# Seventeen of thirty modulation units summed by VectorE straight from the weight ring

## The chip, the cores and the metric

The kernel runs on one core of a Trainium2 chip. The metric is the time of one execution on the device in microseconds (us). Engines are named as in the profile: PE is TensorE, DVE is VectorE, ACT is ScalarE, POOL is GpSimd, SP is SyncE, which issues most of the loads. PEld is PE's loading of weights.

## The reference

All numbers are f32, x has 256 tokens of 1024 channels. Two layers are followed by one block of another kind. Each takes its shifts, scales and gates from one conditioning vector c:

```python
for layer in range(2):
    mod = silu(c) @ w_ada[layer] + b_ada[layer]          # (1024,) @ (1024, 6144)
    sh1, sc1, g1, sh2, sc2, g2 = split(mod, 6)
    h = rms_norm(x, norm1_g) * (1 + sc1) + sh1
    # layer 0: dilated attention (8 heads) beside a gated unit (gMLP); layer 1: a convolution
    # (31 taps) beside stick-breaking attention (8 heads)
    x = x + g1 * (mix(h) @ w_out)
    h = rms_norm(x, norm2_g) * (1 + sc2) + sh2
    x = x + g2 * hierarchical_moe(h)                     # 16 experts of 3 x 2 MB, 2 per token
x = rms_norm(x, final_norm_g)
shift, scl, gate = split(silu(c_2) @ w_c_2 + b_c_2, 3)   # (1024,) @ (1024, 3072)
h = rms_norm(x, g_pre) * (1 + scl) + shift
proj = h @ w_in                                          # (1024, 8192)
# a recurrence and a neighbourhood attention of 16 heads, merged; then
x = rms_norm(x + gate * (merged @ w_o), g_final)
```

## The kernel before

**The ring.** Every large weight is cut into units of 2 MB: 1024 rows by 512 columns, or one of the three matrices of an expert. `stream()` lists all 162 units in the order of loading. SP loads them into a ring of six slots; unit n goes into slot n mod 6, and its load waits until unit n-6 has been read, which PE told with the semaphore `unit_done`. A dense unit is read by `by_channel` (L456) or `by_token` (L469).

**The modulation units.** The three products of a vector with a matrix are 30 such units, ada0 to ada29: ada0 to 11 are layer 0, 12 to 23 layer 1, 24 to 29 the last block. For each, `ada_main` (L492) runs eight matmuls of the conditioning vector, repeated 32 times, against the eight row blocks of the unit, four beside each other in the array; the profile counts an f32 matmul as two instructions, so a unit is x16. ACT copies the bank to SBUF (`ada_part_copy`, L1173). `ada_columns` (L505) then sums over the partitions and turns 512 sums into four columns, by four matmuls of one column each (x8), and DVE adds the bias (`ada_cols`, L1539, `mod<-bank,cv`), which counts `ada_ready` up. PE, ACT and DVE each run their own instructions in the order in which the code stands; a wait holds all that stands behind it.

**Where they stand.** ada0 to 3 come first. ada4 and ada5 are run between the projections ev0, ev1 and ev2 of layer 0. ada6 to 16 are run inside the loop over the eight dilated heads, one in each head and a second in the last ones (from `TWO_A`). Per head PE computes scores (L596, L597), DVE the maximum (L1542 on the bank), ACT the exponential (L1202), DVE sum and division, PE turns the result (L629), ACT copies it (L1231), PE multiplies with the values (L643, L644), ACT evicts the output (L1238). Two banks of scores are in turn, so the scores of head h+2 wait for the output of head h, and ACT runs the exponential of head h+1 before the copy of head h. ada17 to 22 stand in the routing of layer 0 (two behind the projection evo1, four in `experts`), ada23 in layer 1 behind the projection od4, ada24 to 29 in the routing of layer 1.

**Routing and experts.** `routed_norm` and `experts` turn x, compute the logits (L672, L679) and rank the tokens (L691 to L695). Then eight pairs of experts run, each with 192 matmul instructions of 32 columns (L751); they gather tokens (L723) and scatter results (L772).

**POOL** writes a few vectors to DRAM and reads them back in another layout: `broadcast_gate(n)` for the gate of the mixing part, and `affine_by_row(layer)` for scale and shift of the second norm (L2481 and L2484), which `tile_out` (L1125) waits for. The convolution of layer 1 is 31 taps on DVE (L1539, 128x256).

## Time and profile before

| | us |
|---|---|
| median of three runs | 1268.32 |
| lowest, highest | 1265.24, 1273.74 |
| the profiled execution | 1266.25 |
| its span, first to last instruction | 1264.5 |
| PE busy | 1198.5 |
| PE busy with L492 / with L505 | 64.3 / 30.8 |
| DVE busy | 361.2 |
| DMA read | 350.8 MB |

The page cuts the span into 40 slices of 31.6 us. Layer 0 up to its experts takes slices 0 to 6, its experts 7 to 14, the mixing part of layer 1 slices 15 to 18, its experts 20 to 26, the last block the rest.

### The profile page before, as it was taken

The numbers are of one execution on the slowest core, as the hardware profiler recorded it, in microseconds if no ns is written. First come the engines' busy times: TensorE is split into PE (matmuls) and PEld (weight loads), VectorE is DVE, ScalarE is ACT, GpSimd is POOL, SyncE is SP. The second block draws the span as 40 slices with busy tenths as digits, with TensorE's granted clock in tenths as the row PEclk, the third lists the DMA queues.
The fourth block names the chain that finished last, engine by engine and source line by source line (L and its number), as shares of the span: only waits on it lengthen the run. The fifth ranks groups of instructions, "written<-read, shape, count | busy, mean of one in ns | idle before, by whom it ended". The sixth has DMA issues, their size and how long they took to land.

```text
span 1264.5 us, 17438 instructions
## 1 busy us (share of the span) xinstructions
PE 1198.5 (95%) x7154; PEld 702.5 (56%) x7155; DVE 361.2 (29%) x1017; ACT 295.0 (23%) x626; POOL 83.8 (7%) x141
## 2 busy tenths in 40 slices
PE   4799999999999999999889999999999999999997
PEld 1566644544444448764433444445878778767773
DVE  0202414322212123952521121114211344342212
ACT  2112433111000021063400000103002545542101
POOL 2000011000000001500000000000000313200000
PEclk8799999899999999999989999999999999999999
DMA  9997999999999999831889999999834433424000
GB/s 336 313 387 243 308 280 385 382 425 428 430 429 428 429 397 208 247 133 67 360 355 404 404 422 429 427 429 388 204 133 146 152 97 130 150 80 145 17 1 33
DMA packets 90371, 352.77 MB, mean 279 GB/s; under 512 B 5284, under 2 KB 7500, under 8 KB 78028
## 3 DMA queue, kind: packets, MB, share of 16 engines
q1 hardware_dynamic: 83160, 340.68, 71.6%
q0 software_dynamic: 5488, 8.12, 3.1%
q10 hardware_dynamic: 1668, 3.21, 0.7%
q8 instruction: 38, 0.62, 0.2%
q14 instruction: 17, 0.14, 0.0%
HBM read 350.84 MB, written 1.15 MB: 278 GB/s over the span
## 4 chain that ended last, share of the span: by engine, by line
PE 80%; DMA 13%; DVE 2%; ACT 2%; issue 2%; SPq 1%; ACTq 0%; DVEq 0%
PE bank L456 28%; PE bank L751 20%; PE bank L469 12%; DMA ring<-in_moe_w_up 10%; PE bank L723 3%; PE bank L492 3%; PE bank L772 3%; DMA ring<-in_ev_w_in 2%; PE bank L505 2%; PE bank L1016 1%; SPq L368 1%; PE bank L603 1%; PE bank L640 1%; PE bank L643 1%; PE bank L629 1%
## 5 line engine op out<-in xcount | busy, mean ns | idle before, releaser
L456 PE MATMUL bank<-arena,ring 128*128 128x256 f32 x1600 | 356.0, 384 | 6.1 <-DVE arena L1539 2.8
L751 PE MATMUL bank<-ring,arena 128*32 128x512 f32 x3072 | 339.5, 600 | 12.1 <-issue 7.1
L456 PEld LDWEIGHTS bank<-arena,ring 128*128 128x128 f32 x1600 | 305.7, 192 | 54.6 <-issue 7.1
L751 PEld LDWEIGHTS bank<-ring,arena 128*32 128x32 f32 x3072 | 102.0, 111 | 237.0 <-issue 234.3
L469 PE MATMUL bank<-ring,arena 128*128 128x512 f32 x352 | 153.7, 594 | 2.3 <-DVE arena L2378 1.5
L469 PEld LDWEIGHTS bank<-ring,arena 128*128 128x128 f32 x352 | 66.2, 190 | 83.0 <-issue 79.6
L492 PE MATMUL bank<-ring,c_rep 128*32 128x512 f32 x480 | 64.3, 667 | 11.8 <-DMA ring<-in_w_ada 10.1
L2003 DVE TENSOR_TENSOR arena<-arena,bank 128x512 f32<-128x512 f32 x16 | 11.0, 688 | 203.8 <-PE bank L751 203.8
L723 PEld LDWEIGHTS bank<-arena 128*128 128x128 f32 x512 | 60.3, 197 | 13.6 <-issue 13.3
L723 PE MATMUL bank<-arena 128*128 128x128 f32 x512 | 63.4, 284 | 1.6 <-DVE arena L1971 1.5
L1283 ACT ACTIVATE arena<-bank 128x512 f32<-128x512 f32 x16 | 9.6, 597 | 216.8 <-PE bank L751 216.8
L1179 ACT ACTIVATE arena<-bank 128x512 f32<-128x512 f32 x41 | 23.6, 593 | 150.8 <-PE bank L456 121.9
L1539 DVE SCALAR_TENSOR_TENSOR arena<-arena,cv 128x256 f32<-128x256 f32 x144 | 58.3, 476 | 0.3
L772 PE MATMUL bank<-arena 128*128 128x512 f32 x128 | 57.7, 594 | 0.0
L1275 ACT ACTIVATE arena<-bank,mod,gs 128x128 f32<-128x128 f32 x64 | 24.1, 456 | 124.9 <-PE bank L723 124.9
L1542 DVE CUSTOM_DVE_ANT_1 arena<-bank,arena 128x256 f32<-128x256 f32 x32 | 12.3, 423 | 137.4 <-PE bank L604 137.4
L1107 ACT ACTIVATE arena<-x 128x512 f32<-128x512 f32 x20 | 12.5, 626 | 116.0 <-DVE x L1728 99.5
L492 PEld LDWEIGHTS bank<-ring,c_rep 128*32 128x32 f32 x480 | 14.6, 117 | 42.7 <-issue 31.9
L1989 DVE TENSOR_SCALAR arena<-bank,gs,mod 128x128 f32<-128x128 f32 x64 | 21.9, 404 | 50.3 <-PE bank L723 50.3
L772 PEld LDWEIGHTS bank<-arena 128*128 128x128 f32 x128 | 23.2, 191 | 23.0 <-issue 23.0
L1238 ACT COPY arena<-bank 64x256 f32<-64x256 f32 x32 | 11.7, 366 | 99.5 <-PE bank L641 92.2
L1539 DVE SCALAR_TENSOR_TENSOR mod<-bank,cv 128x4 f32<-128x4 f32 (+1 forms) x22 | 3.5, 161 | 101.0 <-PE bank L505 98.8
(300 smaller groups left out, 926.5 us busy)
## 6 DMA issues: line engine op xcount, KB each, us to landing
ring<-in_moe_w_gate SPq DMA_DIRECT2D x32, 2048.0 KB, 14.0
ring<-in_moe_w_up SPq DMA_DIRECT2D x32, 2048.0 KB, 16.7
ring<-in_moe_w_down SPq DMA_DIRECT2D x32, 2048.0 KB, 13.8
ring<-in_w_ada SPq DMA_DIRECT2D x24, 2048.0 KB, 14.1
ring<-in_w_in SPq DMA_DIRECT2D x16, 2048.0 KB, 8.9
ring<-in_w_c SPq DMA_DIRECT2D x6, 2048.0 KB, 9.2
ring<-in_ev_w_in SPq DMA_DIRECT2D x5, 2048.0 KB, 20.2
ring<-in_od_w_in SPq DMA_DIRECT2D x5, 2048.0 KB, 19.6
```

The lines of the kernel that those rows point to most:

```text
L368: eng.dma_start(stage[r % P:r % P + n, r // P, :], src).then_inc(sem(f"{which}_loaded"), 16)
L456: mm = pe.matmul(ps[k0][:, t * S:(t + 1) * S], w[:, k, c:c + P], rhs[:, k, :], start=(k == 0), stop=(k == KT - 1))
L469: mm = pe.matmul(ps[k0][:, :], lhs[:, k, b * P:(b + 1) * P], w[:, k, :], start=(i == 0), stop=(i == KT - 1))
L492: mm = pe.matmul(bank[32 * g:32 * g + 32, :], c_rep[:, n // (2 * ADA_SEG), 4 * r + g, :], w[:, 4 * r + g, :], start=(r == 0), stop=(r == 1 ...
L505: mm = pe.matmul(cols[:, c:c + 1], part[:, c * P:(c + 1) * P], ones[:, 0:1], start=True, stop=True)
L723: mm = pe.matmul(ps[6 + b][:, (k % 4) * P:(k % 4 + 1) * P], xn[:, t, k * P:(k + 1) * P], pick[:, t, :], start=(t == 0), stop=(t == TT - 1))
L751: mm = pe.matmul(bank[col:col + CHUNK, :], lhs[:, k, col:col + CHUNK], ring[:, s0 + e, cut], start=start, stop=stop, tile_position=(0, col))
L772: mm = pe.matmul(ps[2 * t + half][:, :], g_cur[:, t * P:(t + 1) * P], y_pair[:, half * 512:(half + 1) * 512], start=False, stop=True, skip ...
L1179: act.activation(dst, v, func, scale=scale).then_inc(free, 1)
L1275: ins = act.activation(x_cur[:, k, :], ps[6][:, k * P:(k + 1) * P], ACT.Identity, bias=mod[:, sh + k:sh + k + 1], scale=gs[:, 2 * layer + ...
L1539: return dve.scalar_tensor_tensor(out_, in0, scalar, in1, op0, op1)
L1989: ins = dve.tensor_scalar(x_cur[:, k, :], ps[7][:, (k - 4) * P:(k - 3) * P], gs[:, 2 * layer + 1, 0, k:k + 1], mod[:, sh + k:sh + k + 1], ...
```

## The change

Seventeen units (4 to 11, 17 to 23, 28 and 29) are no longer read by PE. DVE reads them in the ring: `modulate` multiplies each of the eight row blocks with its value of the conditioning vector and adds up, eight dependent instructions of 128x512. PE is left with the sum over the partitions, now from DVE's result (`summed_columns`, several units in a row), and DVE adds the bias for several units at once (`summed_cols`). The slot of such a unit is free when DVE has summed it (`read_wait`). The other thirteen units stay with PE: 0 to 3, five in the routing of layer 0 (12 to 16, six before), four in that of layer 1 (24 to 27, six before). The order of loading changes with them: before the experts of layer 0 stand 24 units where there were 30.

```diff
-    u += [("ev", 0), ("ada", 4), ("ev", 1), ("ada", 5), ("ev", 2)]
-    u += [("ev", 4), ("ada", 6), ("ev", 3), ("ada", 7)]
-    u += [("ada", n) for n in range(8, 17)]
+    u += [("ev", 0), ("ada", 4), ("ev", 1), ("ada", 5), ("ada", 6), ("ev", 2), ("ada", 7)]
+    u += [("ev", 4), ("ada", 8), ("ev", 3), ("ada", 9), ("ada", 10), ("ada", 11)]
     u += [("evo", 0), ("evo", 1)]
-    u += [("ada", n) for n in range(17, 23)]
+    u += [("ada", n) for n in range(12, 17)]
     u += [("moe", 0)] * (6 * PAIRS)
-    u += [("od", i) for i in range(5)]
-    u += [("ada", 23), ("odo", 0), ("odo", 1)]
-    u += [("ada", n) for n in range(24, 30)]
+    u += [("od", 0)] + [("ada", n) for n in range(17, 21)]
+    u += [("od", i) for i in range(1, 5)]
+    u += [("ada", n) for n in range(21, 24)]
+    u += [("odo", 0), ("odo", 1)]
+    u += [("ada", n) for n in range(24, 28)]
     u += [("moe", 1)] * (6 * PAIRS)
-    u += [("in", n) for n in (0, 1, 4, 6, 8, 2, 3, 10, 11, 12, 13, 5, 7, 9, 14, 15)]
+    u += [("in", 0), ("in", 1), ("ada", 28), ("ada", 29)]
+    u += [("in", n) for n in (4, 6, 8, 2, 3, 10, 11, 12, 13, 5, 7, 9, 14, 15)]
+SUMMED = tuple(range(4, 12)) + tuple(range(17, 24)) + (28, 29)
-        ROUTE_UNITS = ((17, 6), (24, 6))
+        ROUTE_UNITS = ((12, 5), (24, 4))
-        ROUTE_SOON = 3
+        ROUTE_SOON = (4, 3)
...
+            def summed_columns(lo, hi, base=None):
+                base = lo if base is None else base
+                if lo == base:
+                    pe.wait_ge(sem("ada_ready"), lo)
+                for n in range(lo, hi):
+                    pe.wait_ge(sem("modulation_summed"), summed_at(unit_of[f"ada{n}"]))
+                    part = sum_of(n)
+                    for c in range(4):
+                        o = 4 * (n - base) + c
+                        mm = pe.matmul(ps[4][:, o:o + 1], part[:, c * P:(c + 1) * P], ones[:, 0:1],
+                                       start=True, stop=True)
+                    mm.then_inc(sem("ada_cols_full"), 1)
+                ada[1] = hi
...
+            def modulate(n):
+                at_ = unit_of[f"ada{n}"]
+                dve.wait_ge(loaded[at_ % RING], 16 * (at_ // RING + 1))
...
+                for k in range(KT):
+                    scale = c_rep[:, n // (2 * ADA_SEG), k, 0:1]
+                    if k == 0:
+                        ins = dve.tensor_scalar(part, w[:, 0, :], scale, None, ALU.mult)
+                    else:
+                        step.wait()
+                        ins = stt(part, w[:, k, :], scale, part, ALU.mult, ALU.add)
...
+                ins.then_inc(sem("modulation_summed"), 1)
...
             def after_a(h):
-                ada_columns()
-                if h >= TWO_A:
-                    ada_main()
-            heads(0, 8, "dilated", between_a, after_a, lambda h: ada_main())
-            ada_columns()
+                if h == 2:
+                    summed_columns(8, 10)
+            heads(0, 8, "dilated", between_a, after_a)
...
-            by_token("evo0", oT)
+            by_token("evo0", oT, lambda: summed_columns(10, 12))
...
             by_token("od4", hT, first_scores)
-            ada_main()
+            summed_columns(17, 19)
...
-            ada_columns()
+            summed_columns(19, 21, 17)
...
-            by_token("odo0", oT, order=(4, 5, 6, 7, 0, 1, 2, 3), arrived=convolution_there)
+            by_token("odo0", oT, lambda: summed_columns(21, 22), order=(4, 5, 6, 7, 0, 1, 2, 3),
+                     arrived=convolution_there)
+            summed_columns(22, 24)
...
             by_channel("in4", hT)
+            summed_columns(28, 30)
...
             for t in range(TT):
                 tile_out(2, t)
-            gain(3)
...
+            for n in range(17, 21):
+                modulate(n)
...
+            modulate(21)
+            modulate(22)
+            summed_cols(21, 22)
+            gain(3)
+            modulate(23)
+            summed_cols(22, 24)
...
-            pool.wait_ge(sem("gain_ready"), 4)
             broadcast_gate(1, mod[:, 64:72])
             affine_by_row(1)
+            pool.wait_ge(sem("ada_ready"), 24)
```

How the instructions stand on PE in the last two dilated heads and the start of the projection evo0. L505, L596, L629, L643 and L469 of before are L545 or L559, L651, L684, L698 and L507 of the change. Before:

```order
L492 MATMUL bank<-ring,c_rep 32x512 x8
L596 MATMUL bank<-arena 128x256
L597 MATMUL bank<-arena 128x128
L505 MATMUL bank<-kc,ada_part 128x1 x4
L629 MATMUL bank<-kc,arena 128x128 x3
L492 MATMUL bank<-ring,c_rep 32x512 x8
L643 MATMUL bank<-arena 64x256
L644 MATMUL bank<-arena 64x128
L505 MATMUL bank<-kc,ada_part 128x1 x4
L492 MATMUL bank<-ring,c_rep 32x512 x8
L505 MATMUL bank<-kc,ada_part 128x1 x4
L629 MATMUL bank<-kc,arena 128x128 x3
```

The same place of the change:

```order
L651 MATMUL bank<-arena 128x256
L652 MATMUL bank<-arena 128x128
L684 MATMUL bank<-kc,arena 128x128 x3
L698 MATMUL bank<-arena 64x256
L699 MATMUL bank<-arena 64x128
L684 MATMUL bank<-kc,arena 128x128 x3
L698 MATMUL bank<-arena 64x256
L699 MATMUL bank<-arena 64x128
L507 MATMUL bank<-ring,arena 128x512 x8
L559 MATMUL bank<-kc,arena 128x1 x8
L507 MATMUL bank<-ring,arena 128x512 x21
```

Nothing but the head's own matmuls is left between scores and output projection, and the columns of ada10 and ada11 stand in the middle of evo0.

On DVE between the convolution's last product and the first addition to x in layer 1, before:

```order
L2272 TENSOR_TENSOR arena<-arena 128x1024
L2184 TENSOR_TENSOR arena<-kc 128x20
L2187 TENSOR_TENSOR arena<-arena,kc 128x20 x2
L1726 TENSOR_TENSOR arena<-bank,gate_bc 128x512
L1728 TENSOR_TENSOR x<-x,arena 128x512
```

And of the change (L1764 and L1586 are `modulate`, L1776 is `summed_cols`, L1797 is L1726 of before):

```order
L2351 TENSOR_TENSOR arena<-arena 128x1024
L1764 TENSOR_SCALAR arena<-ring,c_rep 128x512
L1586 SCALAR_TENSOR_TENSOR arena<-ring,c_rep,arena 128x512 x7
L1764 TENSOR_SCALAR arena<-ring,c_rep 128x512
L1586 SCALAR_TENSOR_TENSOR arena<-ring,c_rep,arena 128x512 x7
L1776 TENSOR_TENSOR mod<-bank,cv 128x4
L1586 SCALAR_TENSOR_TENSOR gs<-mod,cv 128x8
L1764 TENSOR_SCALAR arena<-ring,c_rep 128x512
L1586 SCALAR_TENSOR_TENSOR arena<-ring,c_rep,arena 128x512 x7
L1776 TENSOR_TENSOR mod<-bank,cv 128x8
```

Three sums and the gain of the second norm now stand there, in an order that PE's columns must keep up with.

## Rows read from the trace of the kernel before

**Rows 1.** The page: busy time of two engines, and PE's granted clock in 40 slices.
```profile
PE 1198.5 (95%) x7154; PEld 702.5 (56%) x7155; DVE 361.2 (29%) x1017; ACT 295.0 (23%) x626; POOL 83.8 (7%) x141
...
PEclk8799999899999999999989999999999999999999
```

**Rows 2.** What PE waited for, 46 to 640 us: total, times, longest.
```profile
PE bank L751 <- DMA ring<-in_moe_w_up: 1.8, 4, 0.5
```

**Rows 3.** The chain that ended last: start, us, what; layer 0.
```profile
95.66 0.80 PE bank L505 x8
...
112.58 1.85 PE bank L492 x16
...
177.98 25.00 PE bank L469 x58
...
221.56 2.77 PE bank L505 x24
```

**Rows 4.** Timeline of one dilated head, all engines: start, us, engine, line.
```profile
149.59 0.80 ACT L1202 ACTIVATE arena<-arena,small 128x256 f32<-128x256 f32 x2 [2.34 <-DVE small L1760]
150.41 0.48 ACT L1231 COPY arena<-bank 128x384 f32<-128x384 f32 x1
...
150.94 0.65 PE L643 MATMUL bank<-arena 128*64 128x256 f32 x2
...
151.30 0.55 DVE L1779 TENSOR_SCALAR arena<-arena,small 128x256 f32<-128x256 f32 x2
...
151.84 0.36 ACT L1238 COPY arena<-bank 64x256 f32<-64x256 f32 x1 [0.19 <-PE bank L644]
...
152.72 0.70 PE L596 MATMUL bank<-arena 64*128 64x256 f32 x2
...
153.57 0.55 PE L629 MATMUL bank<-kc,arena 128*128 128x128 f32 x3
153.68 0.42 DVE L1542 CUSTOM_DVE_ANT_0 arena<-bank,arena 128x256 f32<-128x256 f32 x1 [0.69 <-PE bank L597]
...
154.56 0.80 ACT L1202 ACTIVATE arena<-arena,small 128x256 f32<-128x256 f32 x2 [2.35 <-DVE small L1760]
```

**Rows 5.** Stretches: from:to, us, busy of PE, PEld, DVE, ACT, POOL, granted clock, DMA share, GB/s.
```profile
139.00:178.00 39.00, 36.49 (x276) 21.25 (x273) 13.73 (x70) 14.08 (x34) 5.54 (x8) 1.00 1.20 298
...
221.00:224.40 3.40, 3.40 (x34) 2.91 (x27) 1.47 (x12) 0.59 (x1) 0.68 (x2) 1.00 0.94 283
224.40:234.80 10.40, 10.26 (x48) 7.11 (x48) 4.58 (x22) 1.03 (x3) 0.00 (x0) 0.51 1.01 357
...
630.70:634.10 3.40, 0.09 (x1) 0.00 (x0) 3.16 (x13) 0.29 (x1) 0.00 (x0) 0.99 1.02 424
634.10:641.00 6.90, 6.12 (x32) 1.75 (x36) 0.95 (x2) 0.00 (x0) 0.00 (x0) 0.51 0.99 420
```

**Rows 6.** DVE by shape: the nearest to a summing step; busy us, mean ns.
```profile
L1539 DVE SCALAR_TENSOR_TENSOR arena<-arena 128x512 f32<-128x512 f32 x2 | 1.4, 685 | 20.3 <-ACT arena L1179 20.3
...
L2149 DVE TENSOR_SCALAR arena<-arena,small 128x512 f32<-128x512 f32 x2 | 1.0, 544 | 0.0
```

**Rows 7.** Timeline of DVE, layer 1: start of the convolution, and the rank in the routing.
```profile
495.20 0.69 DVE L1539 SCALAR_TENSOR_TENSOR arena<-arena 128x512 f32<-128x512 f32 x1 [20.34 <-ACT arena L1179]
...
622.47 0.17 DVE L1918 COPY arena<-bank 128x16 f32<-128x16 f32 x1 [2.82 <-PE bank L695]
```

**Rows 8.** Timeline of POOL and ACT, layer 1: the trip through DRAM, and who needs it.
```profile
492.05 0.91 POOL L2481 DMA_DIRECT2D affine_rows_dram<-gs  x1 [0.48 <-issue]
...
508.05 0.55 POOL L2484 DMA_DIRECT2D mod<-affine_rows_dram  x1
...
600.48 1.50 ACT L1125 ACTIVATE arena<-bank,mod,gs 128x128 f32<-128x128 f32 x4 [2.29 <-PE bank L531]
...
604.89 0.63 ACT L1107 ACTIVATE arena<-x 128x512 f32<-128x512 f32 x1 [2.90 <-DVE x L1728]
```

**Rows 9.** A stretch in which POOL's trip through DRAM of layer 0 runs, columns as in group 5.
```profile
157.00:163.00 6.00, 5.65 (x46) 3.37 (x49) 1.52 (x10) 1.91 (x5) 0.00 (x0) 1.00 2.38 65
```

More of the change, by code:

```diff
@@ L191, in program @@
         neg_ge, neg_ones = at(82, P), at(82.5, P)
-        route_part = [at(32 + 2 * n, HW) for n in range(6)]
+        route_part = [at(32 + 2 * n, HW) for n in range(5)]
         gate_diag, logit_parts = at(44, D), at(48, S)
@@ L257, in program, with done_at, summed_at, copied_at @@
         unit_of = {f"{kind}{i}": n for n, (kind, i) in enumerate(units) if kind != "moe"}
+        def done_at(n):
+            return sum(not summed_unit(u) for u in units[:n + 1])
+        def summed_at(n):
+            return sum(summed_unit(u) for u in units[:n + 1])
+        def copied_at(n):
+            return sum(m not in SUMMED for m in range(n + 1))
+        def read_wait(eng, n):
+            if summed_unit(units[n]):
+                eng.wait_ge(sem("modulation_summed"), summed_at(n))
+            else:
+                eng.wait_ge(unit_done, done_at(n))
+        def sum_of(n):
+            if n < 12:
+                return at(67 + 2 * (n % 4), HW)
+            if n < 2 * ADA_SEG:
+                return at((70, 76, 78, 80)[(n - 17) % 4], HW)
+            return (at(54, HW), ada_part[:, :])[n - 28]
         def full_at(eng, name, b):
@@ L427, in weights @@
             def weights():
+                while summed_unit(units[unit[0]]):
+                    unit[0] += 1
                 n = unit[0]
@@ L478, in ada_main @@
                 ada[0] += 1
+                while ada[0] in SUMMED:
+                    ada[0] += 1
                 bank, _ = ada_place(n)
@@ L684, in experts @@
                     ada_main()
-                pe.wait_ge(sem("ada_part_taken"), units_before + 4)
-                for n in range(ROUTE_SOON):
+                pe.wait_ge(sem("ada_part_taken"), copied_at(units_before + units - 2))
+                for n in range(2):
                     ada_columns()
@@ L697, in experts @@
                 ada_main()
+                for n in range(2, ROUTE_SOON[layer]):
+                    ada_columns()
                 pe.wait_ge(sem("over_ready"), layer + 1)
@@ L841, in experts @@
                 scatter(PAIRS - 1)
-                for n in range(units - ROUTE_SOON - 1):
-                    ada_columns()
                 unit[0] = first + 6 * PAIRS
@@ L1263, in experts @@
                 gate_row(gate, 1)
-                ada_part_copy()
+                for n in range(ROUTE_UNITS[layer][1] - 4):
+                    ada_part_copy()
                 act.wait_ge(sem("route_max_ready"), 2 * layer + 2)
                 act.activation(rt[:, 48:50], rt[:, 48:50], ACT.Exp).then_inc(sem("route_exp_ready"), 1)
-                for n in range(ROUTE_UNITS[layer][1] - 4):
-                    ada_part_copy()
+                ada_part_copy()
                 def tokens_taken(j):
@@ L1706, in ada_cols, with summed_cols @@
                    .then_inc(sem("ada_ready"), 1)
+            def modulate(n):
+                at_ = unit_of[f"ada{n}"]
+                dve.wait_ge(loaded[at_ % RING], 16 * (at_ // RING + 1))
+                dve.wait_ge(sem("setup_ready"), 4 if n >= 2 * ADA_SEG else 1)
+                w, part = ring[:, at_ % RING, :].rearrange("p (k c) -> p k c", c=512), sum_of(n)
+                for k in range(KT):
+                    scale = c_rep[:, n // (2 * ADA_SEG), k, 0:1]
+                    if k == 0:
+                        ins = dve.tensor_scalar(part, w[:, 0, :], scale, None, ALU.mult)
+                    else:
+                        step.wait()
+                        ins = stt(part, w[:, k, :], scale, part, ALU.mult, ALU.add)
+                    if k < KT - 1:
+                        step(ins)
+                ins.then_inc(sem("modulation_summed"), 1)
+            def summed_cols(lo, hi):
+                cols[0] = hi
+                dve.wait_ge(sem("ada_cols_full"), hi)
+                dve.tensor_tensor(mod[:, 4 * lo:4 * hi], ps[4][:, 0:4 * (hi - lo)], cv[:, 4 * lo:4 * hi], ALU.add)\
+                   .then_inc(sem("ada_ready"), hi - lo)
             def route_cols(layer, lo, hi):
@@ L2018, in experts @@
                 left_over(layer)
-                route_cols(layer, 0, ROUTE_SOON)
+                route_cols(layer, 0, ROUTE_SOON[layer])
                 tokens_taken(0)
```

83 lines of the change are left out of this document (42 added, 41 removed).

## The prediction

> **What bounds the kernel now.** Read first the busy shares [rows 1]: PE 95%, DVE 29%. Then what PE waited for [rows 2]: between 46 and 640 us only 1.8 us on weights in flight, so PE and what it exchanges with DVE and ACT set the time, and the ring does so only at the end of the experts. Last the chain that ended last [rows 3]: it runs through PE nearly everywhere, and a modulation unit stands in it with 1.85 us for its matmuls and 0.80 to 0.92 us for its columns (2.77 us for three). Seventeen units off PE are 17 x 1.85 = 31.5 us, 2.5% of the span. The columns stay. The question is how much of the 31.5 us was cover for something else.
>
> The sum is made against the profiled execution: 1264.5 us span, 1.75 us around it, 1266.25 us, which is 2.07 us under the median; that is added at the end. About 12.7 us, 1% of the median, is what a measurement of this kernel tells from no change.
>
> **The summing on DVE.** No row shows an instruction that reads the ring on DVE. The nearest are the same two operations on 512 f32 of SBUF [rows 6]: 0.685 us for the multiply-add and 0.544 for the product, and 0.04 us between dependent ones, as from 150.42 on in the head. One unit: 0.544 + 7 x 0.725 + 0.04 = 5.7 us, seventeen 96 us. DVE has them free, but they stand in its order. Bounds: 4.5 us (all at 0.544) and 8.
>
> **Up to the dilated heads: -2.3 us.** Two matmul units leave (3.75), two more columns come (1.6 to 1.85, up to 8 of them beside 95.66 in [rows 3]), and one hand-over to DVE goes (0.15). DVE sums ada4 to 6 after its part of ev0 at 63 us and is ready near 80, ada7 near 88; PE asks for them at 84 and 93.
>
> **Heads, at full clock: -16.0 us.** Behind ev4 the unit at 112.58 goes, but ACT's copy of the turned scores, which ran under it, is now waited for: -1.5. From head 3 on read one head in the timeline [rows 4]. ACT ends an exponential at 150.39, copies until 150.89, PE multiplies with the values until 151.84, ACT evicts until 152.20, PE computes the next scores from 152.72 until 153.64, DVE takes the maximum until 154.52, ACT ends the next exponential at 155.36. That is 4.97 us, and each step needs the one before it. The unit's matmuls in it lie beside the copy and cost nothing; only the columns (0.47 between 152.2 and 152.7) lengthen it. So without the units a head takes 4.5 us, not 2.3, which is PE's own work. Two heads lose 0.5 us each, the one with the gated unit 0.7, and the columns of ada8 and 9 cost 1.0 more in head 2 than what stood there. The exponential of head 6 then ends 2.3 + 1.5 + 0.2 = 4.0 us earlier, at 151.4 instead of 155.4. One head more, 155.9, then DVE's division (1.45, from 150.42 to 151.85), the turn (0.5), copy (0.5), values (0.9), eviction (0.4): evo0 starts at 159.7 instead of 177.98 [rows 3], 18.3 us earlier. Nearly all of it is the last two heads, where two units each stood on PE.
>
> **PE's clock in the heads: +6.0 us.** [...] In the heads after the change PE works 2.3 of 4.5 us, in matmuls of 128 and 256 columns, where long ones stood between. I take it that the clock falls once there and that nothing so dense comes before evo0 that it rises. [...]
> [...]
>
> **evo0 and evo1: +4.5.** evo0 begins at half the clock; the rows show 6.9 and 10.4 us spells [rows 5], of which part lies in the heads: 5.2 us here cost 2.6. The columns of ada10 and 11 in its middle cost 1.85. DVE sums both only after its last head, from 157.4 to 168.8; PE wants them at 166.8 at full clock, and would wait 1.0 us for the second between the two sets; the slow start hides that.
>
> **Routing and experts of layer 0: -2.1.** Four matmul sets and not five stand before the rank: two at once instead of three (-1.85). DVE's mask becomes the limit near the same time: -1.6. [...] Two sets of columns behind the experts go, beside DVE's norm: 0. Each pair of experts needs 12.6 MB, and PE's wait for it was 1.8 us in all [rows 2]. The first loads now start right behind evo1, but each later one is held by its slot, as before: -0.5. The twelve MB fewer before the experts are worth no more, for the ring wasn't what PE waited for.
>
> **Mixing part of layer 1: +5.0.** One matmul set (-1.85) and one column set (-0.8) leave, seven column sets come (6.45): +3.8. DVE sums ada17 to 20 before the convolution, 4 x 5.7 = 22.8 us, in its 20.3 us of idle time [rows 7]; the excess of 2.1 us meets 1.5 us of idle further on: 0.5 us, hidden by PE. Behind the convolution it sums 21 and 22 until 585, then 23 until 591, and PE asks for them at 583 (21) and 591.5: just in time. If a unit takes 8 us instead, PE waits 5 us here.
> The gain of the second norm now waits for ada21, that is until 585.5 us. POOL's trip through DRAM starts there; before, it took from 492.05 to 508.6 plus about 5.5 us until the last load landed, 22 us [rows 8]. It ends at 608; `tile_out` of ACT, now at 604.3, must begin by 607 to be over before ACT's square at 608.7. +1.2, bounds 0 and 2.5. While that trip runs, the ring gets 65 GB/s instead of 390 [rows 9], so the units 25 to 27 and the first experts land up to 9 us later; they have about 10 us.
>
> **Routing of layer 1: +0.5.** Two matmul sets go, but DVE waited for PE's rank only 2.8 us [rows 7], so at most 1.6 us are gained, and the stretch with small matmuls alone grows from 3.9 to 5.7 us, which speaks for a second fall of the clock: bounds -1.6 and +4. **Last block: +1.85.** The columns of 28 and 29 stand between in4 and in6, where PE is bound; DVE's 11.4 us for the sums are beside in0 and in1.
>
> **The sum.** -2.3 -16.0 +6.0 +4.5 -2.1 +5.0 +0.5 +1.85 = -2.6 us: 1263.7 of this execution, 1265.7 as a median. I give 1265.
>
> **The rivals.**
> First: the clock stays up in the heads. For it: before, it never fell there, nor in the stick-breaking heads of layer 1, which have short matmuls too. Against it: those keep PE busy all the time. Then the 6.0 and 2.6 us stay gained and 1.0 is lost to the wait in evo0: 1258, and 1254 if the fall in the routing of layer 0 is missed too.
> Second, on the other side: the ring is starved in layer 1. Two trips of POOL through DRAM and its forty short loads for the last block move from a stretch with time to spare (475 to 523 us) to 550 to 620 us, where the loads of the routing and of the first experts go out. I count 9 us of delay for the one trip and 10 us of room. If the short loads take as much again, the first pair of experts waits 9 us, and the kernel takes 1265.7 + 9 = 1275. It decides from the point at which up-weights of pair 0 land later than 7 us after its start. For it: the 2.38 of DMA share in [rows 9], a queue held by tiny writes. Against it: the loads themselves are asked for earlier than before.
> Third: DVE takes 8 us a unit. Then PE waits 5 us behind odo0 and 5 in evo0, and some 2 before the heads: 1277. Against it: the rows of the same operation agree within 10 ns.
> Fourth: nothing is seen, because the 31.5 us were all cover: 1268. The last two heads speak against that.
>
> **Chances.** Forecast (clock falls in the heads) 0.6, first rival 0.2, second 0.08, third 0.05, fourth 0.07. The forecast's own range is 1258 to 1272, from the bounds of its terms. With half of the first rival and the second reaching in, 8 in 10 lie between 1253 and 1274. Faster by over 1% (under 1255.6): some 0.6 of the first rival and 0.15 of the forecast, if the routing gains too: 0.22. Slower by over 1% (over 1281): 0.05. The rest, 0.73, is within 1%.
>
> **What would show it.** PE's granted clock about 0.5 somewhere between 135 and 165 us; 4.5 us per head at full clock, 5.8 at half; evo0 starting near 165; no DVE busy time over 6 us a unit; PE waiting for DVE in evo0 for less than 2 us; POOL's second load landing near ACT's first L1125 of layer 1. I am wrong if the heads run much under 4.5 us each, if the clock stays up, or if PE waits for the ring in the experts of layer 1 longer than before.

## The result, and the profile after

| | before | after |
|---|---|---|
| median, us | 1268.41 (20 runs) | 1278.13 (20 runs) |
| lowest, highest | 1264.84, 1273.74 | 1270.53, 1289.81 |
| the profiled execution, its span | 1266.25, 1264.5 | 1287.33, 1285.7 |

The change makes the kernel slower: 1.007 times the time before, 95% interval 1.005 to 1.0091. It was predicted at 1265, with 1253 to 1274 as the range. The ratio leaves out two of the 20 executions after, 1289.64 and 1289.81 us, which count as slow (over 1.5% above the fastest); the median of the other 18 is 1276.2. The times after scatter over 19 us where those before scatter over 9, and the profiled execution is one of the long ones, 9 us over its median. The runs of 1284 us and more had a mean granted clock of 0.950 to 0.956, those under 1273 one of 0.961 to 0.964.

Busy time and clock of the changed kernel, from the page, as in [rows 1]:

```profile
PE 1191.8 (93%) x6882; PEld 709.3 (55%) x6883; DVE 456.7 (36%) x1147; ACT 285.5 (22%) x609; POOL 84.9 (7%) x141
...
PEclk9799788999999989979889999998999999999999
```

PE has 272 matmul instructions less, seventeen units' x16, but only 6.7 us less busy time where 31.5 were taken off; much of the rest went into matmuls at the lower clock: the stretches with a granted clock of 0.50 add up to 113 us, with PE busy for 85.8 of them, against 54 and 43.8 before. The span is cut below at events on PE, each the start of its first matmul (for odo1 the end of its last). "Placed" is the version e2, which comes with the experiments: the same work, its code only elsewhere.

| stretch, us | before | after | placed (e2) |
|---|---|---|---|
| start to ev0 | 46.6 | 48.0 | 47.2 |
| ev0 to evo0 (the dilated heads) | 131.4 | 120.7 | 119.2 |
| evo0 to the first expert | 59.2 | 61.4 | 61.4 |
| experts of layer 0, to od0 | 236.3 | 241.1 | 238.1 |
| od0 to the end of odo1 (mixing part of layer 1) | 129.9 | 144.5 | 136.3 |
| to the first expert | 31.5 | 33.0 | 33.8 |
| experts of layer 1, to in0 | 245.6 | 251.1 | 240.9 |
| in0 to the end | 384.0 | 385.9 | 382.7 |

So the 12 us of the heads are there, and are lost again in the two tails of the experts and in layer 1. The tails, from the last expert's matmul to od0 and to in0, lie inside the stretches of the experts: 9.4 and 12.0 us before, 14.2 and 16.5 after, 9.4 and 12.0 in e2. The chain that ended last, after, shows where PE stands still (start, us, what):

```profile
168.68 9.05 PE bank L507 x16
...
467.38 3.87 issue
471.25 58.01 PE bank L494 x256
...
642.85 5.83 issue
...
650.56 3.76 issue
...
896.18 3.64 issue
899.82 43.26 PE bank L494 x192
```

And the same view of the kernel before, at the same places, which [rows 3] doesn't reach:

```profile
473.50 55.49 PE bank L456 x256
...
630.79 4.08 issue
...
664.42 2.97 issue
...
880.50 55.49 PE bank L456 x256
```

"issue" is time in which PE waits for nothing that the profile shows. At 467.38 ACT has written the last operand, the weights of od0 have been there for 14 us (they landed at 452.9), and PE begins 3.87 us later. Before the change no such row stands ahead of either first projection. What PE's sequencer did in the meantime is seen by asking for the line of the branch behind the experts, which jumps past the code for tokens that are left over (min/median/max in ns, first and last start). After:

```profile
L907 PEldq COMPARE_BRANCH  x2: 6194/6206/6217, 464.9 to 893.5; - x2
```

Before:

```profile
L852 PEldq COMPARE_BRANCH  x2: 349/396/443, 471.9 to 878.7; - x2
```

The same branch takes 0.35 to 0.44 us before and 6.2 us after, in both layers. Some of it lies beside the norm; 3.87 and 3.64 us stand in the chain. The tails are longer by more than that, 4.8 and 4.5 us: before, od0 begins when ACT has written five of its eight pieces (0.92 and 0.81 us of ACT in the chain, where the change has 0.92 and 1.86), and behind the late branch it can't. It is instructions that the branch waits for. The page lists a queue of instruction loads ("q8 instruction: 37, 0.61 MB", 16 KB each); I take it for PE's, because in the straight code of the last block its loads keep step with PE: between the one at 909.8 and the eleventh after it, at 1236.5 us, the trace has 2816 instructions of PE, 256 to a load. Such a stretch of code, 256 instructions, is called a piece below. In the trace one load starts at 468.6, 3.7 us after the branch began, and the branch ends 2.5 us behind that start. Before, one starts at 468.8, which is 3.1 us ahead of the branch. The fourteen profiles of this case agree: they have 2250 branches of PE; 32 of them take 1.39 to 7.95 us, and each of the 32 ends 2.4 to 2.8 us behind the start of such a load; the others take 0.54 us at most, and no load starts in them. Leaving a piece doesn't always bring a load, though: the loop over the experts runs from 257.9 to 468.6 us without one, and a pass is some 490 of PE's instructions and jumps past the two bodies that it doesn't use, so nearly two pieces' worth of code at the least stays there, an estimate from these counts.

PE's granted clock falls more often too, 14 times against 9. Stretches of the changed kernel (columns as in [rows 5]):

```profile
155.51:168.68 13.17, 8.95 (x27) 4.92 (x25) 8.20 (x30) 4.01 (x10) 0.07 (x1) 0.50 0.02 1
...
469.54:476.36 6.82, 5.11 (x12) 4.15 (x13) 6.54 (x10) 0.00 (x0) 0.00 (x0) 0.50 1.05 388
548.04:561.70 13.66, 13.66 (x48) 11.08 (x47) 6.89 (x17) 4.20 (x9) 0.92 (x1) 0.50 0.34 117
...
892.79:903.03 10.24, 5.15 (x16) 4.18 (x17) 8.97 (x20) 3.51 (x10) 0.00 (x0) 0.50 1.05 384
```

The second begins while PE stands at the branch. The fourth begins 0.7 us ahead of the branch, in PE's idle time beside the norm, where the kernel before has a fall too (876.4 to 879.8 us) that is over when in0 starts at 880.5; in the change it lasts 3.2 us into in0. They cost the projections behind them another 2.5 us (58.01 against 55.49) and about 1.7. The kernel before in two of these places:

```profile
469.54:476.36 6.82, 5.75 (x37) 5.02 (x37) 4.75 (x19) 4.53 (x12) 0.92 (x1) 1.00 1.05 387
544.00:558.00 14.00, 14.00 (x82) 9.91 (x82) 8.93 (x23) 7.79 (x17) 0.00 (x0) 1.00 0.83 300
```

### The profile page after: what moved, and what is told of

The parts are those of the page before. It is cut to its first block, busy times and chain, and to the rows that moved or that the text cites. A ratio compares the mean times of both kernels' runs of the same rounds, so it can differ in the third digit from the quotient of the medians.

```text
span 1285.7 us, 17011 instructions
## 1 busy us (share of the span) xinstructions
PE 1191.8 (93%) x6882; PEld 709.3 (55%) x6883; DVE 456.7 (36%) x1147; ACT 285.5 (22%) x609; POOL 84.9 (7%) x141
## 4 chain that ended last, share of the span: by engine, by line
PE 74%; DMA 16%; DVE 4%; ACT 3%; issue 3%; SPq 1%; ACTq 0%; DVEq 0%
PE bank L494 28%; PE bank L808 18%; DMA ring<-in_moe_w_up 13%; PE bank L507 11%; DMA ring<-in_ev_w_in 2%; PE bank L780 2%; PE bank L829 2%; DVE arena L1586 1%; PE bank L1067 1%; PE bank L559 1%; PE bank L532 1%; SPq L404 1%; PE bank L698 1%; PE bank L658 1%; PE bank L695 1%
## 5 line engine op out<-in xcount | busy, mean ns | idle before, releaser
L494 PE MATMUL bank<-arena,ring 128*128 128x256 f32 x1600 | 361.2, 388 | 17.1 <-issue 10.0
L808 PE MATMUL bank<-ring,arena 128*32 128x512 f32 x3072 | 338.5, 595 | 15.8 <-issue 9.6
L494 PEld LDWEIGHTS bank<-arena,ring 128*128 128x128 f32 x1600 | 309.2, 194 | 66.3 <-issue 15.5
L507 PE MATMUL bank<-ring,arena 128*128 128x512 f32 x352 | 158.2, 606 | 2.8 <-DVE arena L2466 1.5
L507 PEld LDWEIGHTS bank<-ring,arena 128*128 128x128 f32 x352 | 67.3, 194 | 83.3 <-issue 79.1
L1586 DVE SCALAR_TENSOR_TENSOR arena<-ring,c_rep,arena 128x512 f32<-128x512 f32 x112 | 84.2, 752 | 4.0
L780 PE MATMUL bank<-arena 128*128 128x128 f32 x512 | 61.4, 278 | 0.0
L1589 DVE CUSTOM_DVE_ANT_1 arena<-bank,arena 128x256 f32<-128x256 f32 x32 | 12.3, 423 | 136.6 <-PE bank L659 136.6
L1586 DVE SCALAR_TENSOR_TENSOR arena<-arena,cv 128x256 f32<-128x256 f32 x144 | 58.3, 485 | 0.3
L532 PE MATMUL bank<-ring,c_rep 128*32 128x512 f32 x208 | 33.3, 782 | 8.4 <-DMA ring<-in_w_ada 6.2
L1255 ACT ACTIVATE arena<-arena,small 128x256 f32<-128x256 f32 (+1 forms) x48 | 22.4, 482 | 47.1 <-DVE small L1831 47.0
## 6 DMA issues: line engine op xcount, KB each, us to landing
ring<-in_moe_w_down SPq DMA_DIRECT2D x32, 2048.0 KB, 14.6
ring<-in_w_ada SPq DMA_DIRECT2D x24, 2048.0 KB, 18.3
```

The source lines that it names most:

```text
L494: mm = pe.matmul(ps[k0][:, t * S:(t + 1) * S], w[:, k, c:c + P], rhs[:, k, :], start=(k == 0), stop=(k == KT - 1))
L507: mm = pe.matmul(ps[k0][:, :], lhs[:, k, b * P:(b + 1) * P], w[:, k, :], start=(i == 0), stop=(i == KT - 1))
L532: mm = pe.matmul(bank[32 * g:32 * g + 32, :], c_rep[:, n // (2 * ADA_SEG), 4 * r + g, :], w[:, 4 * r + g, :], start=(r == 0), stop=(r == 1 ...
L780: mm = pe.matmul(ps[6 + b][:, (k % 4) * P:(k % 4 + 1) * P], xn[:, t, k * P:(k + 1) * P], pick[:, t, :], start=(t == 0), stop=(t == TT - 1))
L808: mm = pe.matmul(bank[col:col + CHUNK, :], lhs[:, k, col:col + CHUNK], ring[:, s0 + e, cut], start=start, stop=stop, tile_position=(0, col))
L1255: ins = act.activation(p[:, m * S:m * S + width[m]], p[:, m * S:m * S + width[m]], ACT.Exp, bias=small[:, c:c + 1], **kw)
```

## The experiments

Each ratio is against the kernel before, on the same chip, with its 95% interval. Theory A is that the loss is PE's loads of code, Theory B that it is DVE and the ring in the mixing part, as a reader of the stretch table might well think: that part has the largest loss.

**e1 and e2: the code moved.** Waits that are already met stand for padding; two of them make one instruction (e1's 256 waits are 128 instructions in its trace, 0.11 us each). e1 has 128 instructions at the head of PE's program; e2 has 192 more in a body that never runs:

```diff
+            for _ in range(256):
+                pe.wait_ge(sem("constants_ready"), 1)
             pe.wait_ge(sem("kc_loaded"), 16)
...
                     with nc.body(name[3], valid_engines=[pe.engine]):
                         emit(3)
+                        for _ in range(384 * (layer == 1)):
+                            pe.wait_ge(sem("constants_ready"), 1)
```

> The changed kernel with 256 waits on a semaphore that is already up, 128 instructions, ahead of PE's first wait, where PE is idle for 9.5 us; nothing else differs, all code behind them moves by 128 instructions. Theory A (place of the code): the 6.2 us branch behind the experts of each layer (L907 of the change, 0.35 to 0.44 us at the same place before) is a load of instructions; these come in pieces of 256 instructions, so their place decides it. With the shift the target behind layer 0 lies in the piece after the one that the loop ends in and should be there, 6.2 us become under 1 and the fall of the clock at 469.5 goes too (2.5 us); behind layer 1 it should still be missed; the 3.8 us stop behind the entry of pair 0 of layer 1 goes: 12 us less than the change, near 1266 to 1270. Theory B (the loss is DVE's and the ring's in the mixing part): the branches are hidden elsewhere and the time stays at 1278.

> As the one before, and 192 more such instructions in the body for a pair of three splits in layer 1, which this input never runs, so that they cost no time and move only what stands behind. Theory A: now both branches behind the experts are under 1 us, and both clock falls behind them are gone or shorter; 18 to 20 us less than the profiled execution of the change at 1285.7 us, a median of 1260 to 1265. Theory B: no different from the change, 1278.

Measured: e1 1262.48 us, ratio 0.9962 (0.994 to 0.9984); e2 1262.25, 0.9945 (0.9925 to 0.9966), and all six runs of e2 lie between 1261.27 and 1262.97. In e1 the branch behind layer 0 takes 0.35 us and that behind layer 1 5.8, as expected; its median is 4 us under the range expected. In e2 the row reads:

```profile
L911 PEldq COMPARE_BRANCH  x2: 343/347/351, 464.1 to 875.1; - x2
```

16 us between the changed kernel and one that does the same work with its code elsewhere (1.25% by the two ratios): Theory A stands so far, though these edits move all the code behind them and so don't say which place in it counts; e12 does. What is left for B is the mixing part's 6.4 us of e2 in the table. The medians don't follow the branches one by one: e1 misses the second branch, its tail there is 16.3 us against e2's 12.0, and its median is only 0.2 us over e2's.
```diff
-pe.br_cond(pe.snap(split_reg) > 0, f"late_pe{layer}", f"on_pe{layer}").branch_hint(ahead)
+pe.br_cond(pe.snap(split_reg) <= 0, f"on_pe{layer}", f"late_pe{layer}").branch_hint(ahead)
```

> The changed kernel with the condition of the branch behind the experts turned round, so that the hint that stands ahead of it names the place that is really gone to; no instruction is added. [...] Theory A with the place alone at fault: 6.2 us each as in the change, 1278. Theory B: 1278.

Measured: 1281.22 us, 1.0105 (1.007 to 1.014). The branch behind layer 0 takes 0.45 us now, with the load of code 6.5 us behind the hint; that behind layer 1 still 6.2, with the load 3.6 us behind the branch. The turn helped in one of the two places only. In the profiled execution (span 1275.4) layer 0's tail is back at its length of before, 9.4 us. The median should by that have been some 7 us better than the change's and isn't; neither 1264 nor 1278 came out as expected, and why is open (its six runs had a granted clock of 0.951 to 0.959, the change's 0.950 to 0.964).

**e4 and e11: the kernel before, moved.** e4 has 64 instructions at the head of PE's program, e11 has 140 and 130 in bodies that never run.

> The kernel before with 64 instructions of waits ahead of PE's first, in its idle time; the computation is that of the kernel before. Theory A: behind the experts of layer 1 the target now lies two pieces on from the branch and is missed: 6 us and up to 3 us of clock more, 1274 to 1278, the size of the loss that the change was to explain, without the change; behind layer 0 it may go either way. Theory B: 1268, as before.

> The kernel before with 140 and 130 instructions in the bodies for three splits of the two layers, which never run. Its branches behind the experts are under 1 us as they stand and should stay so; the leave from the first pair of layer 1, 4.6 us, should fall under 1, and with it the fall of the clock at 668: 1262 to 1265 against 1268.6. That is the measure for what the change itself is worth with code placed well in both. If place does not matter in the kernel before: 1268.6.

Measured: e4 1265.29 us, 0.9976 (0.9957 to 0.9996); e11 1265.36, 0.9976 (0.9955 to 0.9997). e4 missed its expectation: both branches behind the experts are met, and the leave from the first pair of layer 1 takes 2.2 us where it took 4.6. In e11 that leave is under 0.5 us, as expected, and the time just over the 1262 to 1265 that was. The kernel before is thus 3 us off the best of these placings, and had the two branches behind its experts right as it stood.

**e5: what the change took away behind the experts.** The kernel before has two sets of columns between the hint and the branch, 32 instructions; e5 puts 32 back in their place and keeps the code behind at its place modulo 256. A1 is that the missing 32 keep the load from starting ahead of the branch: then both branches come under 1 us, 1264 to 1268 by my estimate. A2 is that the place alone decides.

```diff
                 scatter(PAIRS - 1)
+                for _ in range(64):
+                    pe.wait_ge(sem("constants_ready"), 1)
                 unit[0] = first + 6 * PAIRS
```

> The changed kernel with 32 instructions of waits that are already met put behind the last scatter of each layer, where the kernel before has two more sets of columns (32 instructions) and the change has none; other such waits, in PE's first idle time and in a body that never runs, keep the code from the branch on at the same place, modulo 256, as in the change. [...] Theory A2 (the place alone decides): the place is the one of the change, both branches stay at 6.2 us, 1276 to 1280.

Measured: 1276.9 us, 1.0068 (1.0043 to 1.0093). Its 224 instructions of padding at the head proved too many to hide: ev0 starts at 53.4 us and not at 48.0, so 5.4 us are the padding's own. The branches:

```profile
L913 PEldq COMPARE_BRANCH  x2: 446/3188/5929, 468.9 to 884.3; - x2
```

Layer 0 is met, with a load 7.4 us behind the hint and 2.3 ahead of the branch, which stands at the place modulo 256 at which the change misses. That is as A1 has it. The padding that keeps the place of the branch moves the hint and the loop ahead of it by 32 instructions, though, and no run separates the two. Layer 1 is missed all the same. Neither A1 nor A2 holds alone.

**e7 and e9: more branches placed.** Only padding in bodies that never run.

> The changed kernel with the code placed otherwise: nothing ahead of PE's first wait, 144 instructions in the body for three splits of layer 0 and 172 in that of layer 1, neither of which runs. Both branches behind the experts should be met, as in the well placed version, and the leave from the first pair of layer 0 too, which that version misses (3.9 us; 0.3 in the change): 3 to 5 us less than its 1262.25, near 1258; the entry to the pair of one split in layer 1 stays a miss of 6 to 8 us. If place is not what decides, 1262 or 1278.

> The changed kernel with nothing ahead of PE's first wait; 128 and 116 instructions in the bodies for three splits of the two layers and 54 in the body for left-over tokens of layer 0, none of which runs. Theory A: four of PE's five far branches are then under 1 us, both behind the experts and both leaves from the first pair (3.9 and 2.3 us in the version with two placed), only the entry of layer 1 stays at 6 to 8: a median 3 to 6 us under 1262.25, 1257 to 1260. Rival: what is saved in the branches behind pair 0 is given back by the clock, which falls for one spell more or longer (13.6 instead of 6.8 us in the routing of layer 0 in the version before): 1262.

Measured: e7 1262.62 us, 0.9959 (0.9937 to 0.998); e9 1266.46, 0.9972 (0.9943 to 1.0002). Both expectations, near 1258 and 1257 to 1260, were missed. Both versions gain the 3.4 us of the leave from the first pair of layer 0, and neither median shows it. In e7 the clock then falls for 13.7 us in the routing of layer 0 (6.8 in e2), and that stretch is 3.7 us longer. In e9 the branch behind layer 0 takes 6.2 us again, though by my count its place modulo 256 and its distances are those of the next version, e10, which meets it. So the rule by which I placed the code is not complete. e9's profiled execution also has PE's clock at half from 546.0 to 552.9 us, as the change has at 548.0.

**e12: no branch.** The code for left-over tokens, which this input doesn't use, is left out on PE, and with it the branch and its hint; 115 instructions in each of two bodies that never run keep the code of layer 1 at its place modulo 256 to one instruction.

```diff
-                pe.br_cond(pe.snap(split_reg) > 0, f"late_pe{layer}", f"on_pe{layer}").branch_hint(ahead)
-                with nc.body(f"late_pe{layer}", valid_engines=[pe.engine]):
-                    left_over_tokens(layer)
-                nc.switch_bb(f"on_pe{layer}")
```

> The changed kernel without PE's branch behind the experts: the code for tokens that are left over, which it jumps past and which this input never needs, is left out on PE, so the program goes straight on. 115 instructions in each of the bodies for three splits, which never run, keep the code of layer 1 at its place modulo 256 to one instruction. Theory A: the loss in the change is this branch: 3.9 and 3.6 us of stop and the 2.5 and 1.7 us of half clock behind them go, and nothing else; entry and leave of pair 0 of layer 1 stay as in the change (7.7 and 3.8 us). 12 to 16 us under the change, 1262 to 1266. Theory B (the two versions that place the code gained by something else): 1275 to 1278.

Measured: 1266.77 us, 0.9982 (0.9966 to 0.9998), 11.4 us under the change by the medians, 11.2 by the two ratios with 3 to either side; 12 to 16 were expected. The tails of both layers are at 9.4 and 12 us as in the kernel before. That is the price of the far branch in the change, reached by taking the branch out and not by placing it; the entry to the experts of layer 1 stands still for 10.7 us in its chain, 1.1 more than in the change.

**e8: DVE's sums behind the convolution.** Three units get two of their eight steps.

```diff
-                for k in range(KT):
+                KN = 2 if 21 <= n < 24 else KT
+                for k in range(KN):
```

> The well placed version with DVE's sums of ada21 to ada23 cut to two of their eight steps, which leaves out three quarters of three units: DVE is through with them 12 to 13 us earlier. Theory of the prediction (DVE is just in time behind the convolution, the trip through DRAM costs 1 to 2 us): only PE's waits of 0.4 and 2.0 us and what hangs on them go, 2 to 3 us less than 1262.25. Rival (DVE's sums are what makes the output projection of layer 1 5 us longer): 5 us or more less, 1257.

Measured: 1264.22 us, 0.9975 (0.9952 to 0.9998); the median tells nothing, as its runs scatter from 1259 to 1271. The stretch does: odo0 to the end of odo1 takes 31.3 us against 33.7 in e2. 2.4 us is what DVE's sums cost there, the "2 to 3" of the prediction's theory. The next stretch, to the first expert, is 3.0 us longer than in e2 (36.9 against 33.9), so the execution as a whole is no shorter for it. In e2 the rows on it read (ACT, then PE, timeline):

```profile
603.64 1.51 ACT L1180 ACTIVATE arena<-bank,mod,gs 128x128 f32<-128x128 f32 x4 [6.81 <-DMA mod<-affine_rows_dram]
...
607.68 1.06 PE L586 MATMUL bank<-kc,arena 128*128 128x128 f32 x8 [1.96 <-ACT arena L1193]
```

ACT waits for POOL's trip through DRAM, which ends at 603.6, and PE's turn of the second tile is 2.0 us late for it. For DVE itself PE waits 0.4 us (584.57, columns of ada23).

**e6 and e10: PE's clock in the heads.** Eight matmuls of 32x512, whose result is thrown away, stand between the turn and the values, where the kernel before had a unit: in heads 3 to 7 (e6), in heads 1 to 7 (e10, whose edit is shown). If they keep the clock up, I put e6 at 1255, with evo0 5 to 6 us ahead of e2's 166.4 and evo 2 us faster, and e10 at 5 to 7 us under its twin e9, with evo0 4 to 6 us ahead; if the clock falls all the same in the 6 us behind ev3, e10 at 2 to 3 us under e9. These are estimates.

```diff
+            def filler(h):
+                if h:
+                    pe.wait_ge(sem("ada_ready"), 8 if h < 3 else 10)
+                    for r in range(2):
+                        for g in range(4):
+                            pe.matmul(ps[4][32 * g:32 * g + 32, :], c_rep[:, 0, 4 * r + g, :],
+                                      hT[:, 2 * g:2 * g + 2, :], start=(r == 0), stop=(r == 1),
+                                      tile_position=(0, 32 * g))
-            heads(0, 8, "dilated", between_a, after_a)
+            heads(0, 8, "dilated", between_a, after_a, filler)
```

> The well placed version (two branches behind the experts met) with eight matmuls of 32x512 put into each of the dilated heads 3 to 7, between the turn and the values, where the kernel before had a modulation unit; their result is thrown away, and the code behind keeps its place modulo 256. [...] Rival (the heads are bound by PE's own work and not by the clock): the 1.85 us of each filler are paid, evo0 starts 5 us later, 1267.

> As the one before in the placing of its code (with 22 instructions ahead of PE's first wait), and with eight matmuls of 32x512, whose result is thrown away, in each of the heads 1 to 7. [...]

Measured: e6 1266.79 us, 0.9992 (0.9972 to 1.0012), of which some 6 us are again the padding at its head (ev0 at 53.3). That is the number of e6's rival, but not its mechanism: from ev0 to evo0 e6 takes 117.1 us against 119.2 in e2, so the matmuls are not paid. e10 1257.61, 0.9906 (0.9877 to 0.9936), the fastest version of all, 11.8 us under the kernel before on its chip; 1252 to 1254 had been expected. The heads and the wait ahead of them, e2:

```profile
126.00:166.40 40.40, 28.75 (x106) 19.91 (x104) 21.79 (x79) 13.05 (x28) 2.94 (x4) 0.63 0.47 166
...
146.60:151.15 4.55, 2.27 (x12) 1.46 (x12) 2.83 (x12) 1.65 (x4) 0.13 (x1) 1.00 0.02 2
155.50:161.40 5.90, 4.02 (x11) 2.41 (x11) 2.30 (x15) 1.65 (x4) 0.00 (x0) 0.50 0.00 0
```

The same stretch of e10, up to its evo0:

```profile
126.00:163.65 37.65, 33.97 (x223) 18.65 (x223) 21.19 (x79) 13.05 (x28) 2.90 (x4) 0.95 0.49 174
```

A head takes 4.55 us at full clock and 5.90 at half in e2, and 4.5 in e10 with the filler in it (values begin at 145.51, 150.03, 154.53 and 159.04): 1.9 us of matmuls more in each head for nothing. The clock falls once in this stretch, for 3.4 us, and not twice for 17 each. From ev0 to evo0 that is 2.0 us, in evo another 1.5. e10 has one more fall of 3.4 us, at 112.7, ahead of its first filler: ev3's 64 instructions take 15.8 us there and 14.1 in e2. What more e10 gains over e2 has the code's place beside it: 3.9 and 2.3 us at the leaves from the first pairs, which e10 meets. e10 beats its twin e9 by 8.9 us, but e9 misses a branch of 6.2, so what the filler is worth by itself is read from the stretches: 3.5 us, and an estimate of 5.2 if the 1.7 of that other fall are put aside.

## Why the prediction was wrong

**What held.** Up to evo0 the terms were -2.3 -16.0 +6.0 = -12.3; measured -12.2 in e2 and -10.7 in the change, where the clock fell once more at 114.5. e10 tells the terms apart. It pays 1.7 us in ev3 and 1.5 in the gated unit (3.54 us for the 2.05 of before) for its two short falls; without them its 117.2 would be 114.0, an estimate: 17.4 us under before where 18.3 were forecast at full clock, and 5.2 under e2 where 6.0 were forecast for the clock. The head's chain of ACT, DVE and PE was right to 0.1 us (4.5 forecast at full clock, 4.55 measured; 5.8 at half, 5.90). The term of 6.0 stood on the two falls in [rows 5], to 0.51 for 10.4 and 6.9 us, the first behind 3.4 us of small matmuls, the second behind 3.4 us of almost none, and on an estimate of 0.64 us more for the values and for the scores of a head at half clock, 1.3 a head over four to five heads. No run shows the 6.0 itself; the runs showed 1.35 a head (5.90 against 4.55) and the 5.2. The fall of the clock came about where it was put, but twice (138.4 to 148.7 and 155.5 to 172.6, with 6.8 us at full clock between) where the prediction had it stay, and it also lay on the gated unit (3.8 us in e2 for 2.05), which the term of 6.0 didn't count. So "all cover" (fourth rival) and "the clock stays up" (first) are out. From evo0 to the first expert +2.4 was forecast and +2.2 measured in both. The last block: +1.85 forecast, +1.9 measured in the change (in e2 1.3 less than before, without the fall of the clock that the kernel before has at 1197). DVE's unit took 5.9 us for 5.7 (steps of 752 ns busy, rows of the same shape [rows 6] 685), so the third rival is out:

```profile
L1586 DVE SCALAR_TENSOR_TENSOR arena<-ring,c_rep,arena 128x512 f32<-128x512 f32 x112 | 84.2, 752 | 4.0
```

The second rival, the starved ring, is out too: in the experts of layer 1 PE waited for weights 2.1 us in all, in four waits of at most 0.6, against 1.0 before. Longer than before was one of the prediction's signs of being wrong; by 1.1 us it is met, and too small to matter.

```profile
PE bank L808 <- DMA ring<-in_moe_w_up: 2.1, 4, 0.6
```

**What failed.** The step "Two sets of columns behind the experts go, beside DVE's norm: 0", and with it the assumption that a removed instruction has only its own duration. The operands' side was right: the norm hides the sets (tails of 9.4 and 12.0 us in e2, as before). But behind them stands a branch over 368 instructions (a count of the program). It was 0.4 us before, 6.2 after, twice, with the load of code 3.6 and 3.7 us behind it. In the profiled execution it makes the tails 4.8 and 4.5 us longer, with the clock behind it 2.5 and 1.7 more: 13.5 us; e12 puts it at 11.4 by the medians. That the missing sets brought it is borne out in layer 0 only, by e5; in layer 1 e5 has 32 instructions in their place and misses. And e2 meets both branches without them, so what failed is a zero for the place of the code as much as for the sets. The 4.08 and 2.97 us of "issue" at 630.79 and 664.42 stood in the chain of before and I took them as given; they were the sign that PE's program is not always there when PE needs it: the branches at the two places (628.41 and 661.69) take 5.9 and 4.6 us and end 2.5 and 2.4 us behind the start of a load. The change's are 5.83 and 3.76, 2.5 us more.

**What was too small.** Mixing part of layer 1: +5.0 forecast; +6.4 in e2, where 1.96 us are the trip (forecast 1.2, bounds 0 and 2.5), 0.4 DVE and the rest columns and two short falls of the clock (463.9 to 467.3, of which od0 has 1.4 us, and 586.8 to 590.2). In the profiled execution of the change it was +14.6. 1.9 of the difference to e2 are the slow od0 behind the branch; 6.4 are the stretch from od4 to odo0, 53.1 us against 46.7 in e1, e2 and e3, with the clock at half from 548.0 to 561.7. That fall was in no term. e9 has one of 6.8 us there, the other nine profiled versions of the changed work have none. The two that have it are the two whose branch behind layer 0 was missed, some 75 us earlier; with one profile each that is an observation and no proof. It goes into the 1285.7 us of this profile; how much of it is in the median isn't known. Routing of layer 1: +0.5 forecast, bounds -1.6 and +4; +1.5 and +2.3, with the second fall of the clock (630.0 to 636.8) that the upper bound stood for.

**The sum again.** With both branches met the change gives 1262.25 us (e2) against a forecast of 1265. Against the kernel before with its code placed (e11, 1265.36) the change itself is worth about 3 us, 0.3% by the two ratios and as much to either side, and e7 and e9, placed otherwise, have medians of 1262.6 and 1266.5. Within that the forecast of the work was right, and the time was wrong by the place of the code.

**What stays open.** When a hint leads to a load in time. By my count of PE's program, for the branch behind layer 0: target in the next piece of 256 and the piece entered in the loop, met in e1, e2, e7 and e10, missed in e9; target two pieces on, met by the hint before the change, in e4, e3 and e5, missed in the change. The traces tell two ways of being met: 0.44 to 0.46 us with a load ahead of the branch, 6.5 to 7.4 us behind the hint (before, e3, e4, e5, and e10 too; 3.7 in e11), and 0.34 to 0.35 us with no load between hint and branch (e1, e2, e7). The 32 instructions may decide it in layer 0 (e5), not in layer 1. Why e3, with one branch met, is no faster than the change, and e1, with one missed, no slower than e2. Why the clock falls in some executions at 546 to 562 us and not in others. And what brings the fall of the kernel before at 224.4 us: the prediction laid it to the small matmuls ahead of it, but e4 and e11 have the same ones (L505 and the rank, 224.5 to 228.5 and 223.8 to 227.7 us) and a granted clock of 1.00 from 205 to 245.

## What to carry to other kernels

Before taking short instructions away from an engine that is bound, look for what stands behind them: a branch, a load of code, the clock. An "issue" row in the chain of waits can be a price that moves with the code, as the 4.08 and 2.97 us here, 5.83 and 3.76 in the change; so time a change of this kind in two or three placings of its code (e2's padding in a body that never runs has no record in its trace), or a gain of 5 us is drowned in 16 us of chance. Where a change leaves PE idle in short turns beside ACT and DVE, try matmuls in the gaps: here 1.9 us of them in each head cost nothing and kept the clock up but for 3.4 us. Useful ones are better than thrown-away ones.

## What the runs showed of the hardware

- The same instructions at another place in the program: 1278.1 (the change) and 1262.3 us (e2). The six runs of e2 scatter over 1.7 us, the twelve of e1 and of e9 over 15 and 18, the twenty of the change over 19.
- A branch of PE past 368 instructions: 0.34 to 0.46 us with its code there, 5.8 to 6.2 us without (the change, e1, e3, e5, e9), with a DMA share of 1.05 beside it; the load starts 3.3 to 3.7 us behind the branch and the branch ends 2.5 to 2.6 us later. A load starts 6.5 to 6.6 us behind the hint in layer 0 of before, e3, e4 and e10.
- Over the fourteen profiles: 32 branches of PE over 0.54 us, each ending 2.4 to 2.8 us behind the start of a load of 16 KB; in the straight code of the change one load to 256 of PE's instructions.
- The leave from the first pair of experts into hinted code: 0.3 to 0.5 us or 1.4 to 4.6, by version. It differs with the code of that layer at the same place, too: in layer 0 3.9 us in e2, 2.9 in e8.
- 224 instructions of waits that are already met at the head of PE's program: ev0 5.4 us later (e5); 128 of them: ev0 no later (e1 46.9, e2 47.2, the change 48.0).
- DVE's multiply-add of 128x512 with its factor in c_rep and one operand in a ring slot: 752 ns; 685 within the arena. The ring need not be the reason: before the change the same operation at 128x256, outside the ring, takes 476 ns with its factor in the tile cv and 421 in the rows that name the arena alone. Which of the two it is wasn't tried.
